# One full-precision matmul of 288 columns ahead of the first down tile of each feed-forward group

## The reference

```
u = rmsnorm(x, g2) @ w_up                   # 1024 -> 4096
x = x + jnp.square(jax.nn.relu(u)) @ w_down # 4096 -> 1024
```

## Time and profile before

| | |
|---|---|
| median of 3 runs | 1340.3 us (1339.67 to 1340.41) |
| the profiled execution | 1340.7 us, of which the span is 1338.9 us |
| PE busy | 1321.1 us, 99% of the span |
| DVE busy | 918.4 us, 69% |
| ACT busy | 616.9 us, 46% |
| granted TensorE clock, mean over the core | 0.999 |

### The profile page before, as it was taken

The page is one execution under the profiler, slowest core; times in us unless marked ns, Lnnn a source line. Parts: engine busy times, 40 slices in busy tenths (PEclk is TensorE's granted clock), DMA queues, the critical chain, the costliest instruction groups (busy, mean ns, idle before and its releaser), DMA issues.

```text
span 1338.9 us, 24739 instructions
## 1 busy us (share of the span) xinstructions
PE 1321.1 (99%) x10083; PEld 1286.0 (96%) x10083; DVE 918.4 (69%) x1455; ACT 616.9 (46%) x1046; POOL 63.4 (5%) x52
## 2 busy tenths in 40 slices
PE   7999999999999999999999999999999999999998
PEld 7999898999999999999999988989999999999998
DVE  7767787789476476476666777777974845846744
ACT  6323334478347156166242333345861742732833
POOL 0000001000000000000610000010000000000032
PEclk9999999999999999999999999999999999999999
DMA  8221220132323232222252222202223322322312
GB/s 236 77 81 59 64 57 32 44 99 95 95 64 126 64 94 94 71 86 94 82 121 70 64 74 54 64 32 80 64 95 95 95 95 64 94 94 63 126 64 72
DMA packets 115631, 110.28 MB, mean 82 GB/s; under 512 B 18830, under 2 KB 109398, under 8 KB 115414
## 3 DMA queue, kind: packets, MB, share of 16 engines
q1 hardware_dynamic: 110256, 105.06, 25.8%
q10 hardware_dynamic: 5286, 3.97, 1.0%
HBM read 105.21 MB, written 3.81 MB: 81 GB/s over the span
## 4 chain that ended last, share of the span: by engine, by line
PE 90%; DVE 6%; ACT 2%; issue 1%; DMA 0%; SPq 0%; ACTq 0%; DVEq 0%
PE psum L1656 56%; PE psum L1961 8%; PE psum L1963 7%; PE psum L1962 7%; PE psum L1709 1%; DVE z L1233 1%; PE psum L1798 1%; PE psum L1918 1%; PE psum L1865 1%; PE psum L1859 1%; PE psum L1925 1%; PE psum L1893 1%; PE psum L1909 1%; PE psum L1829 1%; PE psum L1825 1%
## 5 line engine op out<-in xcount | busy, mean ns | idle before, releaser
L1656 PE MATMUL psum<-hid_h,w_hi 128*128 128x288 f32 x1232 | 267.4, 298 | 0.0
L1656 PE MATMUL psum<-hid_l,w_hi 128*128 128x288 f32 x1232 | 263.7, 295 | 0.0
L1656 PE MATMUL psum<-hid_h,w_lo 128*128 128x288 f32 x1232 | 263.7, 295 | 0.0
L1656 PEld LDWEIGHTS psum<-hid_h,w_hi 128*128 128x128 f32 x1232 | 197.2, 188 | 0.7
L1656 PEld LDWEIGHTS psum<-hid_l,w_hi 128*128 128x128 f32 x1232 | 197.5, 188 | 0.0
L1656 PEld LDWEIGHTS psum<-hid_h,w_lo 128*128 128x128 f32 x1232 | 197.3, 188 | 0.0
L1656 PE MATMUL psum<-xh,w_hi 128*128 128x288 f32 x800 | 178.8, 304 | 2.1 <-ACT x L584 1.9
L1541 DVE TENSOR_TENSOR tmp<-psum,rms 128x576 f32<-128x576 f32 x63 | 47.8, 758 | 185.9 <-PE psum L1656 185.9
L1656 PE MATMUL psum<-xh,w_lo 128*128 128x288 f32 x800 | 172.2, 296 | 0.0
L1656 PE MATMUL psum<-xl,w_hi 128*128 128x288 f32 x800 | 171.9, 296 | 0.0
L771 ACT ACTIVATE w_hi<-stage 128x1024 fp32r<-128x1024 f32 x64 | 67.7, 1058 | 219.0 <-PE psum L1656 218.2
(11 more groups left out here) (339 smaller groups left out, 2635.0 us busy)
## 6 DMA issues: line engine op xcount, KB each, us to landing
stage<-in_w_up SPq DMA_DIRECT2D x32, 1024.0 KB, 5.4
stage<-in_w_down SPq DMA_DIRECT2D x32, 1024.0 KB, 5.0
stage<-in_w_in SPq DMA_DIRECT2D x18, 1024.0 KB, 5.2
stage<-in_w_in SPq DMA_DIRECT2D x16, 256.0 KB, 4.6
stage<-in_w_out SPq DMA_DIRECT2D x8, 512.0 KB, 6.3
stage<-in_w_out SPq DMA_DIRECT2D x4, 1024.0 KB, 5.0
z<-in_x_prompt SPq DMA_DIRECT2D x4, 512.0 KB, 6.3
out<-z SPq DMA_DIRECT2D x3, 512.0 KB, 2.7
```

What stands on the lines that cost most here:

```text
L1656: ins = M(acc[t % 2][:, a, :], lhs(w), mov[:, k, a * HALF:(a + 1) * HALF], start=first and n == 0, stop=last and n == 2)
```

## The change

One line is added, in the branch of `down_tile` for a group's first tile. After the wait for the bank, PE multiplies the constant `ones` (128 by 128) by the first 288 columns of the constant `rconst`, read as F32, and writes the result to the first half of the tile's PSUM area. The next matmul on this area starts a new sum (`start=True`), so what was written is never read.

```diff
@@ -2012,6 +2012,7 @@
                         pe.wait_ge(s_fc, UP * l + 4 * g + 6)
                     else:
                         pe.wait_ge(s_fd, UP * l + 4 * g + 6)
+                        M(acc[tile_m % 2][:, 0, :], ones, rconst[:, 0:HALF].bitcast(F32), start=True, stop=True)
                     for k in range(KT):
                         if i == 0:
                             pe.wait_ge(s_hid, hid0 + 8 * g + k + 1)
```

## The result

The changed kernel takes 1347.03 us (median of 5 runs, 1346.16 to 1347.12) against 1340.3 us before. The ratio is 1.005, with a 95% interval of 1.0038 to 1.0061: slower by 0.5%, where 1336.5 us had been forecast and the range ended at 1344.7. The time is that of the rival to which the prediction gave 0.06, "Plain, and group 0 loses its quick pace too", at 1346.7 us.

What follows compares the result with a forecast made beforehand. PE's gapless matmul stream was taken as the bound; 3.88 − 7.73 = −3.85 us gave 1336.85 from the profiled 1340.7, and 1336.5 us as median. Own range 1335.7 to 1337.4; 8 in 10: 1335.9 to 1344.7.

Steps and rivals of the forecast that it cites:

- Plain, and group 0 loses its quick pace too: Down tiles: groups 1 to 3 stay at 51.19 us, group 0 adds 2.54 us in all; 1346.7 us, chance 0.06.
- The cost of the added matmul: First down tile of each group: eight executions at 0.485 us on PE, nothing hidden, +3.88 us.
- the second term: Down tiles behind the added matmul take 0.1300 instead of 0.1333 us per matmul in six groups; −7.73 us.
- the three quick places: Behind `sum_squares`, the quick pace of 0.1300 us per matmul came at three of four places.
- fourteen of sixteen short runs: Attention part: of 16 runs of 18 F32R matmuls behind full-precision transposes, fourteen took 2.39 or 2.40 us, the plain pace.
- the interruption in the earlier trace: Behind the third `sum_squares`: a matmul due 0.26 us after 685.48 started 0.34 us after; an interruption ends the quick pace.
- the pace stays plain: Down tiles of the six plain groups do not quicken, only the 3.88 us cost is left; 1344.2 us, chance 0.30.
- slower: Whole kernel: a measured time more than 0.2% (2.7 us) above the kernel before; chance 0.35.
- the plain rival: Down tiles of the six plain groups keep 0.1333 us per matmul; 1344.2 us, slower by 0.29%, chance 0.30.

Runs made afterwards that it cites:

- the two-matmul kernels: Kernel before plus two full-precision matmuls of 288 columns ahead of groups 1 to 3's first down tiles: banks 4 and 5, 1338.69 us; bank 4 alone, 1338.17 us.
- that of the second tile: Kernel before plus two F32R matmuls of 128 columns ahead of the second down tile of groups 1 to 3; 1334.93 us, ratio 0.9959.

## Why the prediction was wrong

**What bounds the kernel** was read rightly. PE's stream has no gap, and the time of each of the five kernels that were timed in rounds is within 0.5 us of what its expectation worked out for the pace that was then found.

**The cost of the added matmul** was right: 0.485 us forecast, 0.48 to 0.49 measured, nothing hidden.

**The step that failed** is the condition of the second term: "If the added matmul does what `sum_squares` does, the down tiles take the quick pace where they had the plain one." It does not. The term of −7.73 us came out as zero, and group 0, of which the text says that it "has its quick pace already and gets the cost alone", paid 2.54 us more. The term's size was about right: with two matmuls in place of one, 6 × 0.97 − 7.73 = −1.9 us was worked out and −1.8 and −2.4 us measured (1338.69 against 1340.48, 1338.17 against 1340.59). In detail, its 0.11 us for the last tile didn't come (5.57 us as before), and the 0.77 us between the layers were not in it.

**Why it failed.** The prediction had the right facts and weighed them wrongly. It named the difference, one instruction against two, and that "what phase a single one leaves no row tells". It still took the three quick places as evidence for a kind of instruction, when all three showed the same count. A count of one had not been seen at all, and the nearest rows, fourteen of sixteen short runs at the plain pace, spoke against it. The starts add what no count could tell: the single matmul does shift the stream, from the second plain state to the first, which has the same pace.

**The chances of the rivals** were also off. The loss in group 0 got 0.06 with the plain pace elsewhere, as if it were a second mishap. The two are close to one fact: if an inserted instruction only shifts the state of the stream, a third one behind the two can undo what they did as easily as one alone can fail, and the runs show both. All 29 probes that met a quick stream ended it. The row that came nearest to saying so is the one on which the prediction leaned for the opposite, the interruption in the earlier trace rows that ended the pace. Given "the pace stays plain", the loss deserved much more than a sixth of the chance, and the range of 8 in 10 would then have had to reach 1347. The chances of "slower" also don't quite add up: 0.30 and 0.06 are already more than the 0.35 given.

**One spacing for each column count.** In the Trainium skill, the page "TensorE: Matmul & The Clock Gate", section "Back-to-back issue gap", gives for a stream of weight loads and matmuls one sustained spacing for each of two column counts, about 81 ns at 128 and about 131 ns at 512, and says that its formula N/2.4 + 2.5 ns is the gap of an isolated matmul. It has no figure for 288 columns and no second spacing for the same instruction. If there were only one, the change would give nothing back and take 1344.2 us, the sum of the plain rival. That is nearer than the forecast, but the trace doesn't bear it out: the same 288 columns run at 130 and at 133 ns at the same granted clock, and with one spacing there is no room for the loss in group 0 nor for the gain of the two-matmul kernels.

**What stays open.** The runs show three states of the stream that last through the down tiles, that inserted instructions shift by a fixed rule, and that come round after four full-precision matmuls behind the pairs. They don't show what in PE holds them, nor why the quick and the plain stream also changed places at the boundary between the layers without an insertion, in some kernels and not in others (37.61 us for the 288 matmuls in three kernels, 38.39 in that of the second tile, which arrived at the same pace). That the phase lies in the hand-over of matmuls and weight loads is only argued. The first plain run, behind the two of `sum_squares` at the start of layer 0, fits "the arriving state decides" but was not tested by itself.

## What to carry to other kernels

Where a long run of equal matmuls bounds the kernel, divide length by count for every piece of the chain: a pace that differs by 2.5% between equal pieces is a gain that no busy share shows. A dummy instruction ahead of the run may switch it, but its effect depends on what arrives, so try counts and sizes (two F32R matmuls of 128 columns were the cheapest of those whose time was compared), keep it away from pieces that have the good pace already, and look again after any edit to the stream ahead. Read the single gaps too: they told apart two plain states that no length showed. And when a trace shows an effect only behind two instructions, it says nothing yet about one.

## What the runs showed of the hardware

Matmuls of 288 F32R columns with a weight load each ran, in the down tiles, at one of two steady paces, 0.1300 or 0.1333 us, at a granted clock of 1.00. At the plain pace one gap in four was 0.140 us, and its position made two plain states. Which state followed an inserted matmul was fixed by the state that arrived and by the form inserted, without an exception in 128 cases. Either pace held over up to 432 matmuls and across tile boundaries with satisfied waits. Behind the pairs the pace went by the number of full-precision matmuls of 288 columns inserted, with a period of four: quick for 2, 6, 10 and 14. One such matmul costs 0.485 us in the stream, 3.6 to 3.7 times an F32R one of the same size, and the switch from one type to the other and back costs at most 0.02 us more (0.50 us from group to group for the single one).
